# Attention steps issued in pairs on TensorE, with maximum and exponential at the even step

## What is computed

```python
def _attend(q, k, v):
    s = jnp.einsum('bqkgd,bskd->bkgqs', q, k).astype(jnp.float32) * (HEAD_DIM ** -0.5)
    p = jax.nn.softmax(s, axis=-1).astype(v.dtype)
    return jnp.einsum('bkgqs,bskd->bqkgd', p, v)
# 8 heads of 64, 2 key/value heads (4 query heads each), queries in blocks of 128;
# latent queries read 256 context and 1024 latent keys, context queries only the context
# (and are computed in layer 0 alone)
```

## Time and profile before

| | |
|---|---|
| median of 3 runs | 2626.99 us |
| the profiled execution | 2627.32 us |
| its span | 2625.4 us |
| PE, DVE, POOL, ACT busy | 98%, 67%, 39%, 33% |
| attention of layer 0 (about 180 to 582 us of the span) | 402 us, PE busy 402.00 |
| attention of layer 1 (about 1640 to 2030 us) | 390 us, PE busy 388.88 |

### The profile page before, as it was taken

How to read it: one execution, slowest core, us unless ns; L and a number is a source line. 1 busy time by engine, 2 the same in 40 slices (tenths; PEclk the granted TensorE clock), 3 DMA queues, 4 the chain that set the end, 5 groups by cost and what they waited for, 6 DMA issues and landing times.

```text
span 2625.4 us, 32561 instructions
## 1 busy us (share of the span) xinstructions
PE 2581.9 (98%) x13236; PEld 2154.9 (82%) x13236; DVE 1761.4 (67%) x1849; ACT 855.4 (33%) x1272; POOL 1020.4 (39%) x883
## 2 busy tenths in 40 slices
PE   7999999999999999999999999999999999999997
PEld 5888888888887888888878788888888888887886
DVE  4756666665219998947658865777773299885756
ACT  3334444444200000035314433555553000005324
POOL 3721221122235333334485763121214455554660
PEclk9999999999999999999999999999999999999999
DMA  6111111111265111124443422111112211114442
GB/s 276 33 67 43 49 48 44 41 51 51 68 223 197 40 34 40 41 79 149 137 146 131 163 72 73 37 45 37 45 37 92 73 50 49 48 44 143 146 133 88
DMA packets 75748, 220.48 MB, mean 84 GB/s; under 512 B 8528, under 2 KB 13904, under 8 KB 74576
## 3 DMA queue, kind: packets, MB, share of 16 engines
q1 hardware_dynamic: 55008, 181.95, 20.4%
q10 hardware_dynamic: 20592, 36.46, 3.7%
HBM read 173.29 MB, written 45.09 MB: 83 GB/s over the span
## 4 chain that ended last, share of the span: by engine, by line
PE 91%; DVE 4%; POOL 1%; ACT 1%; issue 1%; DMA 1%; ACTq 0%; DVEq 0%; SPq 0%; POOLq 0%
PE PS L830 50%; PE PS L1027 21%; PE PS L1068 6%; PE PS L1092 6%; PE PS L1079 5%; DVE e L1979 1%; POOL wl L694 1%; PE PS L934 1%; PE PS L919 0%; DVE Z L2099 0%; PE PS L913 0%; POOL wh L692 0%; DMA vec<-vecs 0%; DVE Z L2073 0%; PE PS L1055 0%
## 5 line engine op out<-in xcount | busy, mean ns | idle before, releaser
L692 POOL CAST wh<-wraw 128x512 fp32r<-128x512 f32 (+1 forms) x394 | 331.3, 841 | 933.7 <-PE PS L830 572.7
L830 PE MATMUL PS<-Uh,wh 128*128 128x512 f32 (+1 forms) x1536 | 572.7, 373 | 6.7 <-ACT Uh L1286 5.5
L694 POOL TENSOR_TENSOR wl<-wraw,wh 128x512 fp32r<-128x512 f32 (+1 forms) x394 | 564.4, 1432 | 31.6
L830 PE MATMUL PS<-Uh,wl 128*128 128x512 f32 (+1 forms) x1536 | 566.4, 369 | 0.0
L830 PE MATMUL PS<-Ul,wh 128*128 128x512 f32 (+1 forms) x1536 | 559.5, 369 | 0.0
L1914 DVE SCALAR_TENSOR_TENSOR cv<-hc,vec,cv 128x1024 f32<-128x1024 f32 x360 | 436.5, 1240 | 8.7
L1879 DVE TENSOR_TENSOR PTl<-PS,PTh 128x512 fp32r<-128x512 f32 x328 | 226.9, 692 | 241.1 <-ACT PTh L1405 239.7
L1027 PE MATMUL PS<-Uh,wh 128*128 128x512 f32 (+1 forms) x960 | 356.0, 371 | 5.1 <-ACT stgP L1592 4.2
L1027 PE MATMUL PS<-Uh,wl 128*128 128x512 f32 (+1 forms) x960 | 356.1, 371 | 0.0
L1027 PE MATMUL PS<-Ul,wh 128*128 128x512 f32 (+1 forms) x960 | 355.5, 370 | 0.0
L830 PEld LDWEIGHTS PS<-Uh,wh 128*128 128x128 f32 x1536 | 291.0, 189 | 60.0 <-issue 9.9
(11 more groups left out here) (171 smaller groups left out, 3765.3 us busy)
## 6 DMA issues: line engine op xcount, KB each, us to landing
wraw<-w SPq DMA_DIRECT2D x156, 512.0 KB, 3.5
graw<-stg ACTq DMA_DIRECT2D x88, 256.0 KB, 2.0
wmB<-wmod SPq DMA_DIRECT2D x32, 512.0 KB, 6.8
e<-graw SPq DMA_DIRECT2D x24, 640.0 KB, 3.9
wraw<-w SPq DMA_DIRECT2D x48, 256.0 KB, 4.1
e<-graw SPq DMA_DIRECT2D x24, 512.0 KB, 3.6
wmA<-wmod SPq DMA_DIRECT2D x8, 1024.0 KB, 17.4
hL<-hT_in SPq DMA_DIRECT2D x8, 640.0 KB, 19.9
```

Of the source, the lines that this page charges most:

```text
L692: nc.gpsimd.tensor_copy(hi[:, s], wraw[par][:, s]).then_inc(whi[par], 1)
L694: nc.gpsimd.tensor_tensor(lo[:, s], wraw[par][:, s], hi[:, s].bitcast(F32), ALU.subtract).then_inc(wsplit[par], 1)
L830: ins = mmul(PS[:, at + c:at + c + m], w[:, k * P:(k + 1) * P], x[:, k, c0 + c:c0 + c + m], start=(first and a == 0), stop=(last and a == 2))
```

## The change

PE now takes steps two at a time. In a pair (kt, kt + 1), kt even, it issues: at kt 8 the transpositions of q, the scores of the next unit's head, the products with V of both steps of the pair before, the eight transpositions of both steps into the two banks, and the gate matmuls of both steps. ACT runs the exponential of head kt / 2 at the even step, behind `PTh` of that step and ahead of `PTh` of the odd one. DVE runs the maximum at the even step as before, but ahead of `PTl`. The copies of q at kt 8 stand ahead of `PTh` and `PTl` of that step. The number of instructions of compute stays the same.

```diff
--- before.py
+++ after.py
@@ -219,7 +219,7 @@
 def exps_at(nk, kt):
     if nk == 2:
         return (0, 1, 2, 3) if kt == 0 else ()
-    return (kt // 2,) if kt % 2 == 1 and kt < 8 else ()
+    return (kt // 2,) if kt % 2 == 0 and kt < 8 else ()
 
 
 def score_at(h, nk):
@@ -1118,11 +1118,9 @@
                         q_fill(1)
                     gate_slice(("p", h))
                 pe.wait_ge(s_kv, 2 * (l + 1))
-                for step, (un, kt) in enumerate(order):
+                for step in range(0, len(order), 2):
+                    un, kt = order[step]
                     nk = units[un][3]
-                    if kt == 0:
-                        pe.wait_ge(s_pn, 4 * (ub + un + 1))
-                    turn_probs(un, kt)
                     if nk > 2:
                         next_q(un, kt)
                     if un + 1 < len(units):
@@ -1130,9 +1128,17 @@
                             scores(un + 1, h)
                     if step >= 2:
                         pv(step - 2)
+                        pv(step - 1)
+                    if kt == 0:
+                        pe.wait_ge(s_pn, 4 * (ub + un + 1))
+                    turn_probs(un, kt)
+                    turn_probs(un, kt + 1)
+                    if nk > 2:
+                        next_q(un, kt + 1)
                     gate_slice((un, kt))
+                    gate_slice((un, kt + 1))
                     if nk == 2:
-                        next_q(un, kt)
+                        next_q(un, kt + 1)
                 pv(len(order) - 2)
                 pv(len(order) - 1)
                 gate_slice(("e", 0))
@@ -1401,10 +1407,12 @@
                 for step, (un, kt) in enumerate(steps_of(l)):
                     nk = units[un][3]
                     bank, n = PT[l, un, kt]
+                    v = q_next(l, un, kt)
+                    if kt == 8 and v is not None:
+                        q_hi(v)
                     act.wait_ge(pt_done[bank], n + 1)
                     fn(PTh[(sb + step) % 3][:], PS[:, PT0[bank]:PT0[bank] + 512], ACT.Copy).then_inc(pt_hi[bank], 1)
-                    v = q_next(l, un, kt)
-                    if nk > 2 and v is not None:
+                    if kt == 9 and v is not None:
                         q_hi(v)
                     if un + 1 < len(units):
                         for h in exps_at(nk, kt):
@@ -1875,16 +1883,18 @@
                     nk = units[un][3]
                     b = (sb + step) % 3
                     bank, n = PT[l, un, kt]
+                    v = q_next(l, un, kt)
+                    if kt == 8 and v is not None:
+                        q_lo(v)
+                    if un + 1 < len(units):
+                        for h in heads_at(nk, kt):
+                            maxes(un + 1, h)
                     dve.wait_ge(pt_hi[bank], n + 1)
                     tt(PTl[b][:], PS[:, PT0[bank]:PT0[bank] + 512], PTh[b][:].bitcast(F32),
                        ALU.subtract).then_inc(pt_free[bank], 1)
                     if un > 0 and kt == 1:
                         o_out(un - 1)
-                    if un + 1 < len(units):
-                        for h in heads_at(nk, kt):
-                            maxes(un + 1, h)
-                    v = q_next(l, un, kt)
-                    if nk > 2 and v is not None:
+                    if kt == 9 and v is not None:
                         q_lo(v)
                     if un + 1 < len(units):
                         for h in norms_at(nk, kt):
```

## The result

The changed kernel takes 2681.7 us (median of 4 runs, 2679.25 to 2684.62) against 2627.2 us for the kernel before beside it: ratio 1.021, 95% interval 1.0198 to 1.0222, so 54.5 us slower. The forecast was 2693 us, 66 us slower, in a range of 2653 to 2721.

The account below looks back on a forecast made before the run. PE, busy 98% of the span, was taken to bound the kernel. To 2627 us came 50 for layer 1's loop and 16 for layer 0's, nothing for the borders: 2693 us, range 2653 to 2721.

Parts of the forecast that it names:

- What bounds the kernel: Whole kernel: TensorE, busy 98%; any us PE waits in either layer's attention adds to the result, nothing behind returns it.
- Part 2, the loop: Attention's scores, maximum, exponential, odd step's copies and normalisation in series make PE wait: 50 us in layer 1, 16 in layer 0.
- One sign: Layer 1's attention, profile after the change: PE not busy for some 50 us.
- The price of the gate copies: ACT, between exponential and odd step's high copy: 0.95 us each, 1.25 of them or 1.2 us a layer 1 unit.
- Part 1, the borders: PE, 328 blocks of four transpositions becoming 164 of eight: no change, bounds no loss and a gain of 8 us.
- The attribution: Part 2, the new order on ACT and DVE, is where the prediction put the cost.
- B: Rival: the odd step's late high copy is hidden and nothing moves, 2627 us (2622 to 2632); chance 0.08.
- C: Rival: borders between transpositions and other matmuls cost, 162 ns at each of 164, and go; 2597 us; chance 0.06.
- D: Rival: the loop also holds in each pair of layer 0 and POOL's doubling comes late, 2735 us; chance 0.06.

Follow-up runs that it names:

- evened pairs: Changed kernel, odd product behind first gate slice, exponential behind both high copies, layer 1 gate copies at odd step, gate slices evened over pairs: 2613.8 us.
- the evened filler alone: Kernel before, PE step by step, with only the table of gate slices evened out over a unit's five pairs: 2638.4 us, ratio 1.0043.
- pairs on PE alone: Changed kernel with the exponential put back to the odd step and the maximum back behind the even step's low part: 2868.1 us, ratio 1.0908.

## Why the prediction was right, and by how much off

**What bounds the kernel**: right. Layer 0's attention grew by 9.6 us (187.0 to 687.4 us of the span before, 185.0 to 695.0 now) and layer 1's by 43.6 (1634.6 to 2019.0 before, 1645.0 to 2073.0 now), 53 of the 55 us by which the span grew; nothing behind gave any back.

**Part 2, the loop**: right in its pieces, and nearly in place. Predicted for layer 1: waits of 2.41 us a unit and 1.2 for gate copies, 3.6 in all. Measured: a unit of 27.64 us, and one without any wait takes 23.87 in the evened pairs, so 3.8. The waits for the output sum, at the scores of the fourth pair and at the last odd product are where they were forecast; the odd product two pairs earlier waits too (0.26 us drawn), and q's transposition waits in 5 units of 14. One sign came out short: PE was to be idle for some 50 us of layer 1's attention, and is drawn idle for 35 (392.96 of 428.00 us busy), for the reason given beside the waits. In layer 0 1.0 was predicted and 30.04 - 29.03 = 1.0 measured. The price of the gate copies (0.95 us, 1.2 a unit in layer 1) is borne out by the kernel that moves them: 22 us, of which 15 x 1.2 = 18 would be layer 1's.

**Part 1, the borders**: this is the term that was mis-sized. I took the border at nothing, with a gain of 0.05 us x 164 = 8 us as the bound. A unit of layer 0 has no waits in the kernel before, and none in the evened pairs, and gets shorter by 29.26 - 29.03 = 0.23 us; one of layer 1 by 24.53 - 23.87 = 0.66, of which 3.3 / 14 = 0.24 was a wait at the scores and some 0.13 that of the products for the output sum (0.58 to 0.62 in place of 0.47), so 0.3. The evened pairs have five borders a unit fewer: 0.05 to 0.06 us each, 0.23 x 16 + 0.3 x 16 = 8 us in all. So the bound was the value. The changed kernel has still fewer borders than the evened pairs, since its four products and its gates of two steps stand together; what the further ones are worth no run shows by itself. The forecast of 2693 was 11.3 us above the measured 2681.7. The borders account for about 8 of these; the waits, 0.1 to 0.2 us a unit longer than forecast, go the other way, and the rest is the shorter units at the start of each layer, which the forecast counted as full ones. The mistake was to price a border from the one gap behind the transpositions (0.39 for four), where the chain shows scores of 1.16 to 1.19 us behind transpositions and of 1.14 in the pairs. Why they are shorter I did not test.

**The attribution**: half right. The loop is the cause, but not because ACT and DVE were reordered. Pairs on PE put four products (0.94 us) between scores and transpositions and want two low parts at once; the early maximum shortens the loop that this closes, from 7.1 us, and doesn't shorten it enough for pairs of 4.6 to 5.1 us. One rival stands: with the pairs PE's scores and products also moved ahead of the transpositions of the even step, where they stood behind them. Pairs with the transpositions first were not run, so what the pairing costs and what this order costs are not told apart.

**Rivals.** B (late copies are hidden) falls with the chain and with the kernel with gate copies moved. C (the borders pay) is right in that they do, at a third of its price (0.05 to 0.06 us where it had 0.162), and wrong in its sum. D (a loop in each pair of layer 0) falls: 1.0 us a unit there. The rule of the Trainium skill quoted for B, in "Perfetto Trace Analysis", "Identifying the Most-Contended Engine", is to judge by occupancy, and TensorE by that of its weight loads; the trace agrees with it on the engine that binds (weight loads 80% of the span, DVE 65%, ACT 32%). What B made of it, that engines of low occupancy may be late for nothing, misleads here: ACT and DVE hold 16% of the chain.

## What to carry to other kernels

When an engine at 98% is fed through two others, add up the loop from its first instruction to the next instruction that waits for the answer, in queue order, and compare it with the distance between the two on the full engine; that sum gave 3.6 us a unit in layer 1 where 3.8 were measured, while busy shares said nothing. Batching on the full engine lengthens that loop by all that is batched; what is short and off the path (a copy of 0.95 us, a product of 0.47) must then be placed so that it stands behind the answer, not ahead of it. Batch first, then cut the loop, then even out the filler: in that order the same idea went from 2% slower to 0.5% faster, though the evened filler alone, without pairs, cost 0.4%.

## What the runs showed of the hardware that was not expected

The normalisation of 128x1280 on DVE takes 0.89 us alone, but up to 1.96 us where POOL was at work when it started. DVE and POOL at the same place in layer 0 of the changed kernel (timeline):

```profile
308.48 1.64 DVE L1859 TENSOR_SCALAR Pr<-Pr,ri 128x1280 f32<-128x1280 f32 x1
```

```profile
307.44 0.61 POOL L692 CAST wh<-wraw 128x512 fp32r<-128x512 f32 x1 [14.54 <-PE PS L1027]
308.14 1.29 POOL L694 TENSOR_TENSOR wl<-wraw,wh 128x512 fp32r<-128x512 f32 x1
309.37 1.21 POOL L692 CAST wh<-wraw 128x512 fp32r<-128x512 f32 x1
```

The one that starts later is the one that takes longer. POOL's low part of a weight (L694) was started before the normalisation and kept its 1.29 us, the normalisation took 1.64 in place of 0.89; POOL's second cast, which started while the normalisation ran, took 1.21 where the first took 0.61. It goes the other way round as well: normalisations that started ahead of a piece of POOL kept their 0.89 us, and the piece, where it started some 0.1 us behind them, took 1.23 to 1.27 us (a cast) or 1.88 (a low part). POOL's copy of q at 1819.42 in the earlier trace rows, 1.74 us, is such a case: it started 0.05 us behind a normalisation, and the median of that copy is 1.03.

The prediction used 1.1 us for the normalisation with its reciprocal everywhere; where POOL is ahead of it, it is up to 1.1 us longer. In the kernel before that happens once in most units, at the last head (1.74 us, 0.02 behind the start of POOL's copy of q).

The other thing is the clock of pairs on PE alone, above: it fell to its lower level again and again in layer 1, where PE's idle pieces ahead of the scores were 2.3 us at most (84.5 us at 42 places in 1700 to 2200 us). In layer 0 of the same kernel they were 1.4 us at most (53.9 us at 44 places in 185 to 690 us), and the clock stayed at 1.00, as it did in the attention of the kernel before.
